# A hybrid streaming trunk step: low parts of kept U products on GpSimd, and row steps in seven of eight early slots

## The reference, cut to what matters

```python
def peer(x, w_q, sub_keys, u_tab, v_tab):          # x (576, 2048)
    ...                                            # top-k keys: 8 heads x 16 experts per token, gate gp
    def block_fn(args):
        xb, ib, gb = args
        hid = jax.nn.gelu(jnp.einsum('td,thkd->thk', xb, u_tab[ib]), approximate=False)
        return jnp.einsum('thk,thkd->td', hid * gb, v_tab[ib])
```

## Time and profile before

| what | value |
|---|---|
| time, median of 3 runs | 4428.61 us (4421.59 to 4431.16) |
| the profiled execution's own time | 4437.7 us |
| its span | 4435.9 us |
| TensorE busy, share of the span | 4280.7 us, 97% |
| VectorE busy | 2552.9 us, 58% |
| GpSimd busy | 2657.0 us, 60% |
| ScalarE busy | 1100.8 us, 25% |
| DMA | 941.53 MB, mean 212 GB/s |

### The profile page before, as it was taken

How to read it: one execution, slowest core, us unless ns; L and a number is a source line. 1 busy time by engine, 2 the same in 40 slices (tenths; PEclk the granted TensorE clock), 3 DMA queues, 4 the chain that set the end, 5 groups by cost and what they waited for, 6 DMA issues and landing times.

```text
span 4435.9 us, 73784 instructions
## 1 busy us (share of the span) xinstructions
PE 4280.7 (97%) x29840; PEld 4208.9 (95%) x29840; DVE 2552.9 (58%) x3551; ACT 1100.8 (25%) x1850; POOL 2657.0 (60%) x1516
## 2 busy tenths in 40 slices
PE   6999999999999999899999888999999999999997
PEld 6999999999999999899888888999999999999997
DVE  6863433322234421699577577777777776677744
ACT  4541000011011100100077122332322332323323
POOL 3555444444445555455743656888787787787863
PEclk9999999999999999999999999999999999999998
DMA  3333222222333443222446677999999998999963
GB/s 112 98 104 107 74 77 76 88 93 88 100 122 120 142 137 102 77 91 86 129 159 201 226 279 286 394 386 387 368 390 389 389 385 332 387 385 367 391 250 119
DMA packets 271697, 941.53 MB, mean 212 GB/s; under 512 B 59984, under 2 KB 101200, under 8 KB 221264
## 3 DMA queue, kind: packets, MB, share of 16 engines
q1 hardware_dynamic: 216144, 535.08, 35.1%
q0 software_dynamic: 55296, 402.68, 22.7%
HBM read 879.12 MB, written 58.55 MB: 211 GB/s over the span
## 4 chain that ended last, share of the span: by engine, by line
PE 80%; DVE 10%; DMA 4%; issue 2%; POOL 2%; ACT 1%; DVEq 0%; SPq 0%; ACTq 0%; POOLq 0%
PE ps L1869 74%; DMA wr<-in_w 3%; PE aux L2024 3%; POOL wl L771 2%; PE aux L2190 1%; DVE ob L1669 1%; DMA gl<-hid_s 1%; PE ps L1901 1%; DVE ti L1591 0%; DVE mrall L1592 0%; DVE ti L1599 0%; DVE cand L1601 0%; DVE sel L1630 0%; ACT wh L1112 0%; DVE sel L1635 0%
## 5 line engine op out<-in xcount | busy, mean ns | idle before, releaser
L771 POOL TENSOR_TENSOR wl<-wr,wh 128x1024 fp32r<-128x1024 f32 x444 | 1066.9, 2403 | 422.8 <-ACT wh L1112 421.5
L1869 PE MATMUL ps<-xp,wh 128*128 128x384 f32 x4544 | 1173.9, 339 | 9.8 <-POOL wl L722 6.8
L1869 PE MATMUL ps<-yp,wh 128*128 128x384 f32 x4096 | 1061.9, 340 | 37.0 <-POOL wl L771 15.0
L720 POOL CAST wh<-wr 128x1024 fp32r<-128x1024 f32 x338 | 369.0, 1092 | 1214.5 <-PE ps L1869 666.5
L1869 PE MATMUL ps<-xh,wh 128*128 128x288 f32 x3296 | 991.4, 301 | 1.6 <-DVE yt L1489 1.6
L1869 PE MATMUL ps<-xl,wh 128*128 128x288 f32 x3296 | 972.5, 295 | 0.0
L1869 PE MATMUL ps<-xh,wl 128*128 128x288 f32 x3296 | 969.1, 294 | 0.0
L722 POOL TENSOR_TENSOR wl<-wr,wh 128x1024 fp32r<-128x1024 f32 x338 | 839.6, 2484 | 27.1
L1869 PEld LDWEIGHTS ps<-xp,wh 128*128 128x128 f32 x4544 | 805.2, 189 | 12.1 <-issue 10.3
L1869 PEld LDWEIGHTS ps<-yp,wh 128*128 128x128 f32 x4096 | 750.7, 190 | 42.1 <-POOL wl L771 17.2
L1869 PE MATMUL ps<-xp,wl 128*128 128x384 f32 x2272 | 762.8, 336 | 0.0
(11 more groups left out here) (295 smaller groups left out, 4382.6 us busy)
## 6 DMA issues: line engine op xcount, KB each, us to landing
wr<-in_w SPq DMA_DIRECT2D x786, 512.0 KB, 4.3
gates_s<-gbuf SPq DMA_DIRECT2D x8, 3072.0 KB, 11.8
gtile<-gates_s SPq DMA_DIRECT2D x32, 768.0 KB, 10.5
qkv<-qkv_s SPq DMA_DIRECT2D x9, 768.0 KB, 4.5
gl<-hid_s SPq DMA_DIRECT2D x32, 192.0 KB, 6.6
hid_s<-gl SPq DMA_DIRECT2D x28, 192.0 KB, 3.9
mg<-in_x SPq DMA_DIRECT2D x4, 1152.0 KB, 12.4
qkv_s<-lo SPq DMA_DIRECT2D x16, 288.0 KB, 3.0
```

Of the source, the lines that this page charges most:

```text
L720: pool.tensor_copy(high[u][:, :, :], wr[u][:, :, :]).then_inc(S["hi_done"], 1)
L771: pool.tensor_tensor(wl[q][:, :, :], wr[r_][:, :, :], wh[q][:, :, :].bitcast(F32), ALU.subtract).then_inc(S["lo_done"], 1)
L1869: mm_ = pe.matmul(ps[slot][:, half, 0:moving.shape[1]], weights[w][:, t, :], moving, start=first and t == tiles_[0] and not more, stop=las ...
```

## The change

GpSimd gets a `kept_low` of its own. In place slot 8g + 3 + d, for g from 0 to 6 and even d, it stands ahead of that slot's gathers and of the low part of its piece, and makes the low part of product d/2 of group g + 1 (28 in all). VectorE no longer makes these 28; the four of group 0 stay there. And the early row steps stand in all slots but those equal to 7 modulo 8: the first in slot 5, 44 of them before slot 56, so that all later ones come ten slots earlier and the last row sum stands in slot 404.

```diff
@@ free_slots
-        if start >= STEADY or start % 3 != 2:
+        if start >= STEADY or start % 8 != 7:
@@ block.gpsimd
+        def kept_low(g, k):
+
+            n = G2 * g + k
+            pool.wait_ge(S["m_hi"], n + 1)
+            pool.tensor_tensor(yp[:, n % (2 * G2), TD:2 * TD], gl[k % 2][:, :],
+                               yp[:, n % (2 * G2), 0:TD].bitcast(F32), ALU.subtract).then_inc(S["m_lo"], 1)
+
         two_products(P_F // 2, 1)
         on(P_F // 2 + 3, HPV)
         for p in range(2 * HPV, N_PIECES):
+            g_, d_ = divmod(p - 2 * HPV - 3, 8)
+            if g_ in range(EARLY - 1) and d_ % 2 == 0:
+                kept_low(g_ + 1, d_ // 2)
             for s, slot_ in enumerate(GATHER_AT):
@@ block.vector
-            collect(HPV + 4 * g, g, lambda d: kept_low(g + 1, d // 2) if d % 2 else None, after)
+            collect(HPV + 4 * g, g, after=after)
```

## The result

The changed kernel takes 4447.48 us in the median of five runs (4438.26 to 4452.81), against 4428.61 us before: a ratio of 1.0039, 95% interval [1.0025, 1.0054]. A second set of five gave 4447.58 us and 1.0044 [1.003, 1.0058]. So it is slower, by 17 to 19 us. The sign was right, and 4447 lies near the lower end of the stated range of 4432 to 4545; the size, forecast as 74 us, was wrong by a factor of four.

A forecast was written before the change was run, and what follows sets the result against it. The prediction took a ring of raw buffers, including GpSimd's work, to bound the early stretch. Laps of 330.0 us against 261.15 gave +69 us, the start +5, so 4428.6 + 74 = 4502.6 us; range 4432 to 4545.

The forecast's parts named there:

- ring of raw buffers: Early stretch: a raw load waits for GpSimd's low part to free its buffer; 5.1 us a slot, TensorE needs 4.19.
- VectorE's relief by 28 low parts: Early stretch: VectorE sheds 44 us of work; at most 18.4 us could come back, taken as 0.
- TensorE's waits for VectorE: Early stretch: waits of 13.0 and 5.4 us before; those for VectorE's `yp` should be gone after the change.
- the fixed part of the lap: Odd buffer's two-slot lap without the raw load's landing: 6.34 us with a gather, 5.09 without.
- the landing of the raw load: Duration of the next raw load in each odd lap: 7.2 us in 19 laps with a gather, 5.3 in seven others.
- the argument by arrangement: Odd raw loads would stand between two gathers, as the chain's loads of 8.11, 8.24 and 8.50 us did.
- the first of the prediction's signs of being wrong: Early stretch: the prediction is wrong if raw loads land in less than 4 us beside gathers.
- TensorE's waits for weights: Early stretch: waits for GpSimd's low parts of weights should grow from 17.9 to over 80 us.
- the 5 us of the start: Slots 3 to 5: GpSimd's first `kept_low` waits for VectorE's gated product, so slot 5's low part ends later; +5 us.
- The old three-slot ring: Rival for the early stretch: the ring keeps its form with laps of 17.7 us; +42 us, 4471; chance 0.22.
- Bandwidth: Rival for the early stretch: DMA bandwidth bounds, only the ten gathers count; 29 us, 4458; chance 0.08.
- The faster case: Rival: GpSimd's idle time hides the additions, TensorE regains 13.0 + 5.4 us; 4410; needs landing below 3.7 us; chance 0.12.

The follow-up runs named there:

- subtraction twice: The full change with each of the 28 GpSimd subtractions made twice, the second behind the first; 4472.52 us, ratio 1.0107.
- kept load early: The full change with the load of each group's first kept product issued two slots earlier on SyncE; 4434.54 us, ratio 1.0018.
- start mended: The full change with the first of the 28 subtractions behind the split of slot 3 instead of ahead of it; 4452.48 us, ratio 1.006.
- Low parts only: The kernel before with the 28 low parts on GpSimd, row steps still in two of three early slots; 4434.56 us, ratio 1.0013.

## Why the prediction was right or wrong

**Right: what bounds, and where nothing happens.** The ring of raw buffers binds before and after, and behind slot 57 every profile takes the same time within 6 us. VectorE's relief by 28 low parts, costed at 44 us of its time, brought nothing to the time, as forecast. TensorE's waits for VectorE vanished and were replaced by waits for GpSimd.

**Right: the fixed part of the lap.** Forecast 6.34 us. The lap of 9.55 less its load of 3.47 is 6.08. The subtraction, taken at 1.0 us between 0.90 and 2.40, takes 1.01.

**Wrong: the landing of the raw load**, the term "I take 7.2, between 8.1 and 6.3". It measured 3.47 us in the lap shown, 4.0 in the mean of the chain, and 3.7 and 4.0 over all odd slots from 9 to 57 of the two profiles. Nineteen laps with 3.7 us too much are 70 us, almost the whole forecast. The term came from loads on the chain, which in the kernel before are the long ones: all odd-slot loads of the kernel before took 5.7 and 5.5 us in the mean. With 5.6 for 7.2 the forecast would have been 44 us instead of 74. The step that failed beyond that is the argument by arrangement: a load issued between two gathers took 8.11 us, so it would again. The gather ahead of it shows that the arrangement alone did not make those 8.11 us. Here is the one issued at 2533.78 in the kernel before, and the one at 2586.47 in the changed kernel. These are the issue rows of windows of 1 us, the last column the us to landing:

```profile
rows<-in_u,expert POOLq DMA_INDIRECT x1, 8.5
```

And in the changed kernel:

```profile
rows<-in_u,expert POOLq DMA_INDIRECT x1, 5.4
```

Both stand about 3.5 us ahead of the load. When the load was issued, at 2537.31 and at 2589.82, the first had 5.0 us to go and the second 2.0. In both places the next gather follows the load by 0.13 us, so neither load had the DMA engines to itself.

That a gather still in flight goes with a long load holds in all sixteen traces. Of their 784 raw loads of slots 9 to 57, those issued with no gather in flight took 3.5 us in the mean (199 loads), those issued while one had less than 2.5 us to go 4.0 (152), up to 4.5 us 5.5 (223), and more than 4.5 us 7.3 (210). A gather issued within 0.3 us behind a load with none ahead of it did not lengthen it: 3.4 us (122 loads) against 3.6 without (77). Behind a gather with more than 4.5 us to go, loads that had another one just behind them took 8.5 us (46) against 6.9 without (164). This is an ordering by what was in flight and not an experiment: load and gather share the DMA engines, so each may also have made the other longer.

The runs say when loads are short. With the subtraction in front of the gathers, loads on the chain take 3.6 to 4.4 us in five of the six kernels of that order, and 4.9 in the one with the earlier kept load. As soon as gathers can be issued while GpSimd would wait anyway, they take 5.6 to 8.0. The wait that I costed as a pure loss also held the gathers back behind the raw load. That is argued from the order of these kernels; which packets stood in whose way on the DMA engines was not shown. With this the first of the prediction's signs of being wrong came true, raw loads of less than 4 us beside gathers, and TensorE's waits for weights grew to 23.9 us and not to over 80.

**Wrong: a cost put at nothing.** The forecast followed SyncE's kept loads only at the start. In each group GpSimd now waits for a late one, a lap of 13.2 instead of 9.6 us. Six of these are 22 us; taking them away gave 13. Had the landing been sized right, the sum would have been 19 x (3.5 + 6.34) + 7 x (3.5 + 5.09) = 247 us, 14 less than before. With these 22 us it comes to 269, where the two profiles have 262.5 and 269.5. So with the right landing and this cost still left out, the forecast, the 5 us of the start included, would have been a gain of 9 us. That the sign came out right owes something to luck: one term was too large, and another was missing.

**Half right: the start.** The +5 us were there, 35.9 against 31.1 us from slot 0 to slot 5 (33.9 against 30.1 in the second profiles). But removing them brought nothing, so they don't belong in the sum.

**The rivals.** The old three-slot ring did not survive, as its counter-argument said. Bandwidth does not bind as that rival had it: 304 GB/s moved, against 353 in the steady stretch, and ten more gathers alone cost 5 to 8 us and not 29. The faster case was priced right as to its condition, a landing below 3.7 us: the ordinary laps came down to 9.55, under two old slots of 10.04. It did not come true. The long laps are a part of why. They are not all of it, since without them the kernel still took 7 us more than the kernel before. What spoke for this rival is clearer in the trace than the prediction had it: of VectorE's 27 subtractions, five overlap no subtraction of GpSimd and took 0.55 to 0.56 us, while the other 22 each end 0.41 to 0.43 us behind a low part that GpSimd was making. So VectorE did shed waits on GpSimd, but they were not what held TensorE in the changed kernel.

**Open.** From slot 0 to slot 100 the two profiles of the changed kernel take 478.5 and 479.7 us, those before 474.6 and 472.2, a loss of 4 to 8 us. The timed runs say 17 to 19. So the profiles account for less than half of the loss. All five profiled executions with this order and seven steps in eight slots (subtraction twice, kept load early and start mended among them) lie 4 to 10 us below the median of their sets. Either the stretch varies from run to run more in this order, 262 to 276 us in the three profiles of the change and the change with its start mended, or being profiled helps it. I can't tell these apart.

## What to carry to other kernels

An instruction moved to an idle engine brings its waits with it. What counts is whether it stands between a buffer's landing and its release; put behind the instruction that releases the buffer, the same work cost nothing here (4424 us, as before, against 4447). Follow every transfer that the new wait depends on to its place of issue. And where a stretch is bound by loads and another has TensorE busy throughout, move optional traffic from the first to the second before moving arithmetic: 17 gathers and row steps fewer in the early stretch were worth 27 us. And size a load from all loads of its kind, not from those on the chain alone, which here were the long ones.

## What the runs showed of the hardware that I had not expected

The duration of a 512 KB load is not a constant to be carried from one order to the next. In the early stretch its mean on the chain went from 3.6 to 8.0 us between orders of nearly the same work. Low parts only moves the same bytes in the same slots as the kernel before: 4.3 against 7.5 us on the chain, 4.7 against 5.8 over all loads. What goes with the duration is how long the gather of 1.05 MB ahead of the load still had to go: 3.5 us with none in flight, 7.3 with more than 4.5 us to go. A gather issued just behind the load did not matter where none was in flight ahead of it. The order with a longer wait on GpSimd had the shorter loads, and a sum over the lap with the old durations was much too pessimistic (74 against 19 us). When an extra that leaves this rhythm alone was put into the lap, the same sum came out: 26 laps of 1.05 us are 27 us, and 25 were measured by the medians.
